# Entries of four feed-forward networks and the sparse mixer: first two tiles updated one by one, products of the rounded part first, three constant products in place of six

## What is computed

```python
def macaron_half_ffn(x, pre_g, post_g, w_gate, w_up, w_down):
    h = rmsnorm_2(x, pre_g)
    h = (jax.nn.silu(h @ w_gate) * (h @ w_up)) @ w_down
    return x + 0.5 * rmsnorm_2(h, post_g)
...
        x = macaron_half_ffn(x, *p["ffn1"])
        x = x + rmsnorm_2(p["mixer"](rmsnorm_2(x, pre_g), *p["mix"]), post_g)
        x = macaron_half_ffn(x, *p["ffn2"])
```

## Time and profile before

| what | us |
|---|---|
| median of 3 runs | 2412.68 |
| lowest and highest of them | 2408.5, 2413.09 |
| the profiled execution | 2415.62 |
| its span, first to last instruction | 2413.8 |
| PE busy in the span | 2186.1 (91%) |
| DVE busy | 1630.8 (68%) |
| ACT busy | 1001.6 (41%) |
| mean granted clock of TensorE | 0.971 |

### The profile page before, as it was taken

One profiled execution on the slowest core, in us unless ns is written; L12 is line 12 of the kernel. 1 busy time (PEld: TensorE's weight loads), 2 busy tenths in 40 slices (PEclk: granted clock), 3 DMA queues, 4 the chain that ended last, 5 costly groups with the idle time before them and its releaser, 6 DMA issues. The chain is left out here.

```text
span 2413.8 us, 40938 instructions
## 1 busy us (share of the span) xinstructions
PE 2186.1 (91%) x16106; PEld 1804.5 (75%) x16106; DVE 1630.8 (68%) x3182; ACT 1001.6 (41%) x1908; POOL 510.1 (21%) x533
## 2 busy tenths in 40 slices
PE   8998999987777777779999999999999898999998
PEld 7987998743333233227999979999999777889998
DVE  6776756876676667646667666667666767658666
ACT  5553535443333333334444354444444563014443
POOL 0000000767777777771000000000000000000000
PEclk9999999999888999999999999999999999899999
DMA  5530454999999999995655423554555332003553
GB/s 203 175 114 19 145 187 149 377 362 407 409 409 409 409 409 406 409 409 187 194 183 182 145 69 121 185 184 149 176 184 184 122 105 62 3 3 119 183 183 110
DMA packets 140464, 509.45 MB, mean 211 GB/s; under 512 B 15985, under 2 KB 16753, under 8 KB 140017
## 3 DMA queue, kind: packets, MB, share of 16 engines
q1 hardware_dynamic: 65968, 237.32, 30.8%
q0 software_dynamic: 73728, 268.47, 28.1%
q10 hardware_dynamic: 576, 1.05, 0.2%
HBM read 505.72 MB, written 1.05 MB: 210 GB/s over the span
## 5 line engine op out<-in xcount | busy, mean ns | idle before, releaser
L228 ACT ACTIVATE weights_high<-weights 128x1024 fp32r<-128x1024 f32 x428 | 451.9, 1058 | 526.7 <-PE ps L267 398.6
L265 PE MATMUL ps<-moving_high,weights_high 128*128 128x256 f32 x2224 | 641.4, 288 | 6.5 <-DVE moving_low L1314 3.3
L240 DVE TENSOR_TENSOR weights_low<-weights,weights_high 128x1024 fp32r<-128x1024 f32 x427 | 523.4, 1228 | 178.9 <-ACT weights_high L228 175.7
L267 PE MATMUL ps<-moving_high,weights_low 128*128 128x256 f32 x2224 | 632.1, 284 | 0.0
L266 PE MATMUL ps<-moving_low,weights_high 128*128 128x256 f32 x2224 | 632.0, 284 | 0.0
L2321 PE MATMUL ps<-v_rows,subkeys 128*128 128x512 f32 x1024 | 491.6, 634 | 140.8 <-ACT subkeys L2405 140.8
L2321 PEld LDWEIGHTS ps<-v_rows,subkeys 128*128 128x128 f32 x1024 | 200.3, 203 | 428.0 <-issue 427.9
L2644 DVE CUSTOM_DVE_ANT_0 u_rows<-u_rows,ps 128x1024 f32<-128x1024 f32 x256 | 308.6, 1219 | 196.4 <-DMA u_rows<-in_peer_u,experts 196.0
L265 PEld LDWEIGHTS ps<-moving_high,weights_high 128*128 128x128 f32 x2224 | 429.2, 193 | 11.8 <-issue 8.9
L266 PEld LDWEIGHTS ps<-moving_low,weights_high 128*128 128x128 f32 x2224 | 429.2, 193 | 0.6
L267 PEld LDWEIGHTS ps<-moving_high,weights_low 128*128 128x128 f32 x2224 | 428.7, 193 | 0.0
(11 more groups left out here) (594 smaller groups left out, 3169.1 us busy)
## 6 DMA issues: line engine op xcount, KB each, us to landing
weights<-in_l_ffn SPq DMA_DIRECT2D x264, 512.0 KB, 4.1
weights<-in_w_in SPq DMA_DIRECT2D x44, 512.0 KB, 3.8
weights<-in_l_in SPq DMA_DIRECT2D x24, 512.0 KB, 4.0
weights<-in_l_rkv SPq DMA_DIRECT2D x24, 512.0 KB, 3.6
weights<-in_w_ckv SPq DMA_DIRECT2D x16, 512.0 KB, 4.2
weights<-in_w_up_pair SPq DMA_DIRECT2D x8, 512.0 KB, 3.5
weights<-in_w_mix_out SPq DMA_DIRECT2D x8, 512.0 KB, 4.4
weights<-in_w_cq SPq DMA_DIRECT2D x8, 512.0 KB, 4.3
```

Source lines behind the costliest of these rows:

```text
L228: act.activation(self.high[:, c % SPLIT, :], self.source(c), ACT.Copy).then_inc(self.rounded, 1)
L240: v.tensor_tensor(self.low[:, c % SPLIT, :], self.source(c), self.high[:, c % SPLIT, :].bitcast(F32), ALU.subtract).then_inc(self.split, 1)
L265: pe.matmul(out, lhs.high, rhs.high, start=start, stop=False)
L267: return pe.matmul(out, lhs.low, rhs.high, start=False, stop=stop)
```

## The change

Four things change at the entry.

1. The first pair is updated tile by tile: multiply tile 0, add tile 0, multiply tile 1, add tile 1, and x is announced after each.
2. The multiplication of pair 1 stands behind the low parts of tiles 0 and 1; before, it stood ahead of them. Its addition stays behind them.
3. PE waits first for a tile's high part and makes the six products that need only that, then waits for the low part and makes the other three. The last tile keeps the old order, and the sums stay where they were.
4. `keep_warm` makes three constant products instead of six, in the mixer and in three networks; `l0_ffn1` has none, as before.

```diff
@@ -412,6 +412,12 @@
         pair = slice(2 * q, 2 * q + 2)
         self.own.settle()
         return self.v.tensor_tensor(self.k.x[:, pair, :], self.k.x[:, pair, :], self.k.xn[:, pair, :], ALU.add)
+
+    def tile(self, t):
+        late = self.k.xn[:, t, :]
+        self.own.did(self.v.tensor_tensor(late, late, self.k.late_scale[:, :], ALU.mult))
+        self.own.settle()
+        return self.v.tensor_tensor(self.k.x[:, t, :], self.k.x[:, t, :], late, ALU.add)
 
 
 class FinalGain:
@@ -2648,7 +2654,7 @@
     k.w.n_split = first + N + SPLIT
 
 
-def late_parts_tensor(k, pe, S, parts, squares, sum_bank, warm=6):
+def late_parts_tensor(k, pe, S, parts, squares, sum_bank, warm=3):
 
     keep_warm(k, pe, warm, 3)
     first_three = [k.w.arrived(pe) for _ in range(3)]
@@ -2664,32 +2670,42 @@
             sums(t // 2 - 1)
         if t == 6:
             sums(3).then_inc(S["sum_ready"], 1)
-        pe.wait_ge(S["parts_ready"], t + 1)
-        for bank, tiles in enumerate(first_three):
-            last = product(pe, k.ps[:, bank, 0:T], tiles[:, t, :], parts[:, t, :], start=t == 0, stop=t == KT - 1)
-            if t == KT - 1:
-                last.then_inc(k.w.used, 1)
+        if t == KT - 1:
+            pe.wait_ge(S["parts_ready"], t + 1)
+            for bank, tiles in enumerate(first_three):
+                product(pe, k.ps[:, bank, 0:T], tiles[:, t, :], parts[:, t, :], start=False, stop=True)\
+                    .then_inc(k.w.used, 1)
+        else:
+            pe.wait_ge(S["high_ready"], t + 1)
+            for bank, tiles in enumerate(first_three):
+                pe.matmul(k.ps[:, bank, 0:T], tiles.high[:, t, :], parts.high[:, t, :], start=t == 0, stop=False)
+                pe.matmul(k.ps[:, bank, 0:T], tiles.low[:, t, :], parts.high[:, t, :], start=False, stop=False)
+            pe.wait_ge(S["parts_ready"], t + 1)
+            for bank, tiles in enumerate(first_three):
+                pe.matmul(k.ps[:, bank, 0:T], tiles.high[:, t, :], parts.low[:, t, :], start=False, stop=False)
 
 
 def late_parts_scalar(k, act, S, src, gain, parts, squares):
     for q in range(4):
-        act.wait_ge(S["x_ready"], q + 1)
         for t in (2 * q, 2 * q + 1):
+            act.wait_ge(S["x_ready"], min(t + 1, q + 2))
             act.activation(parts.high[:, t, :], src[:, t, :], ACT.Copy, scale=k.column(gain, t)).then_inc(S["high_ready"], 1)
         act.activation(squares[:, 2 * q:2 * q + 2, :], src[:, 2 * q:2 * q + 2, :], ACT.Square).then_inc(S["squares_ready"], 1)
 
 
 def late_parts_vector(k, v, S, src, gain, parts, update):
 
-    update.first(0)
-    update.second(0).then_inc(S["x_ready"], 1)
+    for t in range(2):
+        update.tile(t).then_inc(S["x_ready"], 1)
     for q in range(4):
-        if q < 3:
+        if 0 < q < 3:
             update.first(q + 1)
         for t in (2 * q, 2 * q + 1):
             v.wait_ge(S["high_ready"], t + 1)
             v.scalar_tensor_tensor(parts.low[:, t, :], src[:, t, :], k.column(gain, t), parts.high[:, t, :].bitcast(F32),
                                    ALU.mult, ALU.subtract).then_inc(S["parts_ready"], 1)
+        if q == 0:
+            update.first(q + 1)
         if q < 3:
             update.second(q + 1).then_inc(S["x_ready"], 1)
 
@@ -2752,7 +2768,7 @@
                         last = pe.matmul(k.ps[:, X_SUM, P:T], k.const("ones"), last_squares[:, t, :], start=False,
                                          stop=t == 3, skip_group_check=True)
                     last.then_inc(S["x_summed"], 1)
-                late_parts_tensor(k, pe, S, x_parts, squares, 4, warm=0 if final else 6)
+                late_parts_tensor(k, pe, S, x_parts, squares, 4, warm=0 if final else 3)
                 for f in range(1, FT):
                     if f >= 2:
                         pe.wait_ge(S["hidden_ready"], f - 1)
```

## The result

The changed kernel is slower: 2420.48 us against 2413.74 us for the kernel before (medians of 22 runs each), a ratio of 1.0023 with a 95% interval of 1.0016 to 1.003. The forecast was 2410.6 us, and 2420.48 lies outside its range.

What follows compares the result with a forecast made beforehand. TensorE, busy 91% of the span, was taken as the bound, so a change pays mostly by letting it start or go on earlier. -2.64 + 0.6 = -2.04 us against 2412.68 gave 2410.6 us, range 2406.0 to 2415.3.

Steps and rivals of the forecast that it cites:

- part 2: Sparse mixer: DVE 0.6 us late, PE's wait for the fifth split about 2.0 us, stage loses +0.6 us.
- rival 1: Sparse mixer: the new 2.0 us wait drops PE's clock, losing up to 1.9 us; about 2412.5 us, chance 0.13.
- rival 4: Entries: three constants instead of six lose the clock, about 2.7 us an entry; 2418.8 us from three on, chance 0.05.
- Part 1: Three networks with a pending branch: PE starts 1.07 us earlier, a lead of 0.88 each reaches the end, -2.64 us.
- Part 3: First network, where the update is a scaling and there are no constants to drop: price 0.
- part 4: Order of products: 21 more bank changes a stage, taken as 0, upper bound 1.5 us a stage.
- Rival 3: Bank alternation costs 0.03 us a change, 0.6 us in each of five stages: +1.1, or 2413.8 us; chance 0.10.
- Rival 2: The mixer's queue isn't the bound and all four entries gain 0.88: -3.5, or 2409.2 us; chance 0.12.

Runs made afterwards that it cites:

- gates moved: Changed kernel with the sparse mixer's 24-column gate products beside chunks 7 and 8 instead of 5 and 6; 2412.56 us, ratio 0.9994.
- bridge: Changed kernel with four constant products ahead of the sparse mixer's fifth chunk, so PE works through most of its wait; 2497.49 us, ratio 0.9981.
- six constants: Changed kernel with six constant products instead of three at the entries; 2415.22 us, ratio 1.0002.
- later clears: Changed kernel with the sparse mixer's two DVE clears moved from ahead of the reciprocal to behind DVE's sixth result; 2409.82 us, ratio 0.9977.
- multiplication between: Changed kernel with the mixer's two clears moved later and pair 1's multiplication between the low parts of tiles 0 and 1; 2411.36 us, ratio 0.9981.
- old mixer entry: Changed kernel with the old entry in the sparse mixer alone, the networks keeping the new one; 2499.36 us, ratio 0.9982.
- clear of 1280: Kernel before with an extra DVE clear of 1280 columns ahead of the sparse mixer's reciprocal; 2418.97 us, ratio 1.0027.
- mixer alone: Kernel before with the new entry in the sparse mixer only, networks old with six constants; 2511.07 us, ratio 1.0024.

## Why the prediction was wrong

**The step that failed is part 2's +0.6 for the mixer, which takes the new wait at full clock.** It measured 8.42: the delay was 0.59, as forecast, and the clock, which the sum puts at nothing, 7.83. The prediction had this only as rival 1, priced too low and given too small a chance. There it named the mechanism, the place and the row that spoke for it. It then priced the fall "like 3.9 us at half rate, loses up to 1.9". In the profile of the kernel before, the two short low stretches of the recurrent mixer last 3.4 us each (from 1887.1 and from 2023.7 us). The new one lasted some 17 us and cost 7.83. For a stretch with only dense products behind the wait the size was nearly right: 3.4 us and 1.5 us with the gates moved. What I didn't look at is what PE does behind this wait: a product of 24 columns stands behind each three large ones, in two chunks. With the right price rival 1 would have been 2410.6 + 7.8 = 2418.4, on the other side of zero, and the case for "slower". The rows to make me careful were in the same profile: one stretch of 14.3 us at 0.52 and one of 7 us at 0.51, with PE busy in both, and I took neither length as the upper bound.

**The chance of 0.13 was too small.** "The work around this wait is dense" was the argument for 0.13. In the trace a wait of about 2 us stood behind dense products and the clock fell in the changed kernel, in two of its variants and in one of the kernel before. The page "TensorE: Matmul & The Clock Gate" of the Trainium skill, section "HAM oscillation — how this bites in real kernels", says that gaps between bursts of matmuls let the gate close and the burst behind them runs cold. I had used it for the four entries, and there no row shows a fall (rival 4 didn't come about). At the mixer's wait, where I hadn't applied it, the trace agrees with it: the products behind the gap ran at 0.50. The waits that this section of the Trainium skill draws are some 3 to 5 us long. Here 1.84 us was enough.

**Part 1 held.** First product at +1.57 (forecast +1.55), tile 2 at +4.66 (+4.74), the wait for it 0.19 (0.3), the fourth split ready at +11.87 (+11.9). The lead is 0.95 where I took 0.88. `l0_ffn2` and `l1_ffn2` gained 0.95 and 0.94, so it reaches the end of a network as the step said. `l1_ffn1` is the exception. Its entry in the changed kernel:

```profile
1690.39 1.53 PE L396 MATMUL ps<-consts 128*128 128x256 f32 x6 [0.44 <-PEq L2737]
1690.76 0.43 DVE L418 TENSOR_TENSOR x_normed<-x_normed,late_scale 128x256 f32<-128x256 f32 x1 [0.67 <-PEq L2737]
...
1692.33 0.36 PE L2681 MATMUL ps<-moving_high,weights_high 128*128 128x256 f32 x1 [0.41 <-ACT moving_high L2692]
```

DVE begins 0.37 us after PE, where both begin together at the other entries, and the first product comes at +1.94. The distance to the constants near the network's end shrank by 0.57 only. The same 0.37 shows with the bridge, with six constants, with the later clears, with the later gates and with the multiplication between, and not in the kernel with the old mixer entry (0.30 and not 0.67 before the multiplication). DVE's operations there are the same in all of them, so the cause lies outside them; it is open. Together the networks gave 0.95 + 0.57 + 0.94 = 2.46 where I had 2.64.

**Part 2 held up to the clock.** Reciprocal at +14.80 (forecast +14.8), a wait of 1.95 (2.0), PE 0.59 later; and with the clock kept at 1.00 the stage costs 0.59 more (0.6).

**Part 3 and part 4 held.** `l0_ffn1` changed by -0.09. Products that change the bank in every second place are 0.12 apart, and with six constants the networks are at most 0.08 us shorter than before and none is longer, where 21 bank changes at even 0.01 us each would have added 0.21. Rival 3 is out.

**Rival 2 is out** as far as the changed kernel goes: DVE's queue does bind, the mixer lost 0.59. Only with the clears out of the way does the mixer gain (163.18 against 164.43).

**The sum.** My terms gave -2.04. Measured in the traces they give +5.87, and 7.83 of the 7.91 between the two are the clock. The miss against the median is 9.9 us: 1.1 more because the kernel before came out at 2413.74 and not at 2412.68, and 0.9 that no stage accounts for (6.74 by the medians, 5.87 by the stages).

## What to carry to other kernels

When a stage is made to start earlier but its next supplier is on another engine's queue, the lead becomes a wait further on: look for what is queued ahead of that supplier and could run later (here two clears, worth a ratio of 0.9977 together with the change), before taking the lead as a gain or as harmless. Price a new wait on TensorE by what follows it: with 256-column products alone behind it a fallen clock was back in 3.4 us, with gate products between them it took 17. Where the wait can't be shortened, a few constant products in it may help: 1.9 us of them kept the clock here, and the stage was 7.8 us shorter.

## What was not expected of the hardware

- The granted clock fell 1.1 us after PE had resumed (0.6 with the gates later, 0.9 with the clear of 1280, 1.8 with the mixer alone), not during the wait, and stayed at the lower level with PE busy for 14 of 14 us while products of 24 columns stood among those of 256. The same short products at full clock, from 1341.10 in the kernel with later gates, did not lower it.
- A wait of about 2 us doesn't always cost the clock. Waits of 1.84, 1.95, 2.02 and 2.03 us had a fall in their profiled executions, one of 2.25 us had none, and one of 1.13 had none. Each of these is one execution. The means of the runs point to a fall in a share of the executions only, for all but the changed kernel itself.
- The start of DVE at one entry moved by 0.37 us with code that differs elsewhere.
